# A transformer block with expert gather: four token groups of two blocks and a ring of ten tiles, in place of two groups of four and a ring of eight

## The chip, the cores and the metric

The kernel runs on one core of a Trainium2 chip. The metric is the device time of one execution in microseconds (us). PE is TensorE (matmuls; PEld are its weight loads), DVE is VectorE, ACT is ScalarE, POOL is GpSimd, SP is SyncE, which only issues DMAs here. All work is in float32.

## The reference

One transformer layer over 1024 tokens of width 1024, with two sub-layers and a final norm:

```python
h = modulate(rmsnorm(x, g1), shift1, scale1)          # shift, scale, gate from silu(c) @ w_ada
qa, ka, va, qb, kb, vb, ga, gb = split(h @ w_in)
y_sb = stick_breaking_attention(qa, ka, va)           # 8 heads of 64, strictly causal over all 1024
y_sw = sliding_window_sink_attention(qb, kb, vb, sinks)   # 8 heads, this chunk of 64 and the one before
x = x + gate1 * ((sigmoid(ga) * (y_sb @ sb_proj) + sigmoid(gb) * (y_sw @ sw_proj)) @ w_out)

h2 = modulate(rmsnorm(x, g2), shift2, scale2)
sub_s = (h2 @ w_q) . sub_keys                          # 8 heads x 2 halves x 128 keys
experts = top16 of the 16 x 16 sums of both top16s     # 16 of 16384 experts, per head and token
act = gelu(h2 . u[experts]); w = softmax(score) * act
x = x + gate2 * sum(w * v[experts])                    # 8 x 16 = 128 experts per token
out = rmsnorm(x, g_final)
```

Each token reads 128 rows of u and of v (2048 floats together) from a table of 16384 rows in HBM.

## The kernel before

**The gather stream.** Tokens lie in 8 blocks of 128. A block needs 128 gather tiles, 1024 in all. One tile is an indirect DMA on POOL (L498) which brings 128 rows of 2048 floats (1.05 MB: four experts each of 32 tokens) into one of the RING = 8 slots of a ring in SBUF. DVE multiplies the u half with the replicated h2 rows and sums (L1336), ACT applies gelu to two tiles' results (L1053), DVE multiplies with the softmax weight (L1347) and spreads it to a diagonal (L1350), PE adds the weighted v half into the block's output (L844), which frees the slots: POOL waits for `vs_done` before it fills a slot again. At a block's end the result goes through the final norm (L1361 to L1371), and the next block's h2 is replicated (PE L831, ACT L1046).

**The mixer.** Everything up to the scores of the sub-keys is done per group of tokens, GROUPS = 2 groups of GB = 4 blocks (T = 512 tokens). The stages of a group: H (norm and transposes, L531), V (L543), for each of 4 head pairs QK (L651) and then SB, one step per block of keys from the group's last block down to block 0, with both heads of the pair (PE L664, ACT abs, exp, ln at L985 to L995, DVE L1220 and L1237, PE L679 and L684, ACT exp L1003, PE L693, ysb copy L1015); SWP (projections of the sliding window, L724 to L739) and SW (L758 to L785, per block); MG (gates and merge, 8 slices of weights, L567 and L570); OUT (L596, per block, with the second norm and its transposes L580); PREP (queries and scores of the sub-keys, one step for each of 8 heads, L632 and L616). The scores go to HBM, and the selection of the top 16 (`keys`, DVE L1252 to L1312, four chunks of two heads per block) reads them from there; it is published through PE L813 and ACT L1030 and L1032 as the indices of 32 tiles.

Weights stream from HBM once per group. By the arrays' shapes: w_v 2 MiB, w_qk 4 x 1, w_sw 3, the table of slopes 0.75, w_mg 8 x 1.5, w_out 4, w_q 8 x 1 and sub-keys 8 x 0.125, and five broadcast rows of 0.5: 37.25 MiB (39 MB) per group. Three thirds of w_ada (8 MiB each) are read once, in the first group.

**The order.** Every engine runs one queue in order. Its instructions are merged when the kernel is built: each stream (`mixer(g)`, `keys`, `dot_products`, `sums`, ...) yields a due time before each piece, and `interleave` takes the earliest. The unit of due times is one gather tile: tile i is due at i. `Plan` gives the mixer's pieces their due times from costs in us, divided by a rate (1.9 us of mixer work per tile). Group 0 is placed before tile 0 (its PREP starts at -40), group 1 starts at tile 40. By these formulas group 1 has H at 40, V at 54, the first QK at 69, SWP at 231, SW at 258, MG at 291, OUT at 384, PREP from 432 to 508; its scores are first needed for block 4, whose tiles start at 512. ACT holds one set of functions at a time: gelu, exp with ln, and sqrt are three sets, and `Tables.use` (L92) loads another one where the next piece in the merged order needs it.

## Time and profile before

| | |
|---|---|
| median of 3 runs | 3839.58 us (3836.57 to 3844.09) |
| the profiled execution | 3838.94 us |
| its span, first to last instruction | 3837.1 us |
| busy: PE, DVE, POOL, ACT | 2710.1, 2223.6, 1172.6, 718.3 us |
| moved by DMA | 1235.07 MB, mean 322 GB/s |
| gather tiles | 1024 |
| loads of an ACT function set | 182 |

The profiled execution lies 1.8 us above its span and 0.6 us under the median. In the rows further down, a time is in us from the start of the span; "idle before" names what an engine was waiting for; PEclk is the granted TensorE clock as a share of 2.4 GHz; a matmul in float32 shows as two passes, each of them counted. A busy PE need not be at its peak, since ends of matmuls are modelled.

### The profile page before, as it was taken

What the parts mean: (1) busy time and instruction counts of PE and PEld (TensorE: products, weight loads), DVE (VectorE), ACT (ScalarE), POOL (GpSimd) and SP (SyncE); (2) the same over time, 40 slices, a digit from 0 to 9 for tenths busy, and PEclk for the clock granted to TensorE, in tenths of its full rate; (3) what the DMA queues carried; (4) which work ended last, traced back from release to release, by engine and by line L of the source; (5) the groups of instructions that cost most, each with busy time, mean ns of one, the idle gap of its engine ahead of it and who ended that gap; (6) DMA issues with size and microseconds to landing.
All of it is one profiled execution on the core that took longest, in us unless ns stands there. A gap on an engine that the chain in (4) does not pass through costs nothing. (4 is left out here: it accounts for less than half of the span.)

```text
span 3837.1 us, 33329 instructions
## 1 busy us (share of the span) xinstructions
PE 2710.1 (71%) x10216; PEld 879.3 (23%) x10216; DVE 2223.6 (58%) x5731; ACT 718.3 (19%) x1681; POOL 1172.6 (31%) x1033
## 2 busy tenths in 40 slices
PE   4886988877776777867998789655555555555555
PEld 2334433322221222222332233200110110001010
DVE  1113002458664667677776856677767767776755
ACT  1222001211435445131012211200010010001000
POOL 0000000133231333323433333444434434443443
PEclk8987999987898989988999899876777777778777
DMA  6310232699876878969998999999989989998998
GB/s 251 137 61 0 86 119 92 226 388 349 325 304 232 342 282 330 408 247 382 420 419 371 418 379 421 361 421 418 412 325 421 417 352 404 421 412 335 421 421 347
DMA packets 189067, 1235.07 MB, mean 322 GB/s; under 512 B 20348, under 2 KB 34716, under 8 KB 50392
## 3 DMA queue, kind: packets, MB, share of 16 engines
q0 software_dynamic: 147616, 1074.03, 69.2%
q1 hardware_dynamic: 41272, 158.91, 10.7%
q8 instruction: 81, 1.33, 0.1%
q14 instruction: 98, 0.80, 0.1%
HBM read 1208.71 MB, written 24.14 MB: 321 GB/s over the span
## 5 line engine op out<-in xcount | busy, mean ns | idle before, releaser
L498 POOL DMA_INDIRECT arena<-in_uv,idx_r x1024 | 1169.5, 1142 | 2639.3 <-PE pb L844 1727.9
L844 PE MATMUL pb<-arena,dg 128*32 128x512 f32 x4096 | 1288.2, 762 | 826.9 <-DVE dg L1350 826.5
L1336 DVE CUSTOM_DVE_ANT_0 arena<-arena 128x1024 f32<-128x1024 f32 x1024 | 1252.0, 1225 | 423.4 <-DMA arena<-in_uv,idx_r 398.2
L844 PEld LDWEIGHTS pb<-arena,dg 128*32 128x32 f32 x4096 | 225.9, 126 | 1780.3 <-DVE dg L1350 1251.3
L1053 ACT ACTIVATE gl<-dots 128x2 f32<-128x2 f32 x512 | 104.0, 203 | 1830.8 <-DVE dots L1336 1829.8
L1347 DVE TENSOR_TENSOR wv<-gl,gate_r 128x2 f32<-128x2 f32 x512 | 82.1, 160 | 336.2 <-ACT gl L1053 316.3
L92 ACT ACT_TABLE_LOAD x182 | 233.5, 1283 | 175.9 <-DVE dots L1336 142.1
L632 PE MATMUL pb<-arena 128*128 128x512 f32 x512 | 239.5, 614 | 12.0 <-issue 6.0
L567 PE MATMUL pb<-arena 128*128 128x512 f32 x512 | 233.2, 606 | 11.2 <-DMA arena<-in_w_mg 11.2
L831 PE MATMUL pb<-arena,ident 128*32 128x256 f32 x1024 | 98.6, 444 | 79.7 <-ACT arena L1046 75.9
L651 PE MATMUL pb<-arena 128*128 128x512 f32 x256 | 120.9, 622 | 19.3 <-DMA arena<-in_w_qk 19.3
L1220 DVE SCALAR_TENSOR_TENSOR arena<-pb,arena 128x512 f32<-128x512 f32 (+3 forms) x96 | 49.0, 552 | 139.7 <-ACT arena L995 132.1
L596 PE MATMUL pb<-arena 128*128 128x512 f32 x256 | 119.4, 617 | 14.7 <-DMA arena<-in_w_out 12.6
L632 PEld LDWEIGHTS pb<-arena 128*128 128x128 f32 x512 | 95.2, 195 | 150.1 <-issue 142.9
L567 PEld LDWEIGHTS pb<-arena 128*128 128x128 f32 x512 | 95.6, 192 | 145.4 <-issue 145.4
L1350 DVE TENSOR_TENSOR dg<-istack,wv 128x64 f32<-128x64 f32 x512 | 115.6, 226 | 19.4 <-DVE wv L1347 1.6
L1181 DVE SCALAR_TENSOR_TENSOR arena<-arena,pb 128x512 f32<-128x512 f32 x32 | 22.0, 687 | 180.9 <-PE pb L570 180.9
L570 PE MATMUL pb<-arena 128*128 128x512 f32 x256 | 116.1, 602 | 0.0
L679 PE MATMUL pb<-arena,tri 128*128 128x512 f32 (+3 forms) x192 | 85.1, 533 | 3.3 <-DVE arena L1220 3.3
L1252 DVE MAX8 vals<-arena 128x8 f32<-128x128 f32 x128 | 37.0, 289 | 84.5 <-DMA arena<-s_scratch 84.4
L1336 DVE DVE_READ_ACCUMULATOR2_ANT dots<- 128x1 f32 x1024 | 84.5, 83 | 0.0
L724 PE MATMUL pb<-arena 128*128 128x512 f32 x128 | 62.4, 640 | 17.7 <-DMA arena<-in_w_sw 17.7
(153 smaller groups left out, 2111.3 us busy)
## 6 DMA issues: line engine op xcount, KB each, us to landing
arena<-in_w_ada SPq DMA_DIRECT2D x12, 2048.0 KB, 17.5
arena<-in_w_mg SPq DMA_DIRECT2D x16, 1536.0 KB, 10.1
arena<-in_w_q SPq DMA_DIRECT2D x16, 1024.0 KB, 12.4
arena<-in_uv,idx_r POOLq DMA_INDIRECT x1024, 11.9
arena<-in_x SPq DMA_DIRECT2D x16, 512.0 KB, 13.5
arena<-in_w_qk SPq DMA_DIRECT2D x8, 1024.0 KB, 8.2
arena<-in_w_out SPq DMA_DIRECT2D x2, 4096.0 KB, 13.0
s_scratch<-arena SPq DMA_DIRECT2D x16, 512.0 KB, 15.3
```

Source lines behind the costliest of these rows:

```text
L92: self.act.add_instruction(mybir.InstLoadActFuncSet(name=self.nc.get_next_instruction_name(), act_func_set_id=table, engine=mybir.EngineTy ...
L498: pool.indirect_dma_start(ring[:, i % RING, :], None, uv, bass.IndirectOffsetOnAxis(ap=idx_r[:, b % 2, 4 * n + c:4 * n + c + 1], axis=0)). ...
L567: m = pe.matmul(bank, wmg[ft % 2][:, q * KT + k, :], hT[:, k, :], start=(k == 0), stop=(k == KT - 1))
L570: m = pe.matmul(bank, wmg[ft % 2][:, 16 + (q - 2) * 4 + k, :], y[:, k, :], start=(k == 0), stop=(k == 3))
L596: m = pe.matmul(pb[:, BGB + 2 * (j % 2) + i, :], merged[:, k, j * P:(j + 1) * P], wout[:, k, i * HALF:(i + 1) * HALF], start=(k == 0), sto ...
L632: m = pe.matmul(pb[:, BGB + p, 0:T], wq[h % 2][:, p, k, :], h2T[:, k, :], start=(k == 0), stop=(k == KT - 1))
L651: m = pe.matmul(pb[:, BGB + i, 0:T], wqk[p % 2][:, i * KT + k, :], hT[:, k, :], start=(k == 0), stop=(k == KT - 1))
L831: x_ = pe.matmul(pb[32 * q:32 * q + 32, MISC, 256:512], selector(c), h2cur[:, 256 * i:256 * i + 256], start=True, stop=True)
L844: m = pe.matmul(pb[32 * c:32 * c + 32, VACC + i, :], dg[:, n // 2 % 2, c, :], ring[:, (2 * g + c % 2) % RING, D + i * HALF:D + (i + 1) * H ...
L1053: act.activation(gl[:, 2 * (g % 4):2 * (g % 4) + 2], dots[:, 2 * (g % 4):2 * (g % 4) + 2], ACT.Gelu).then_inc(gelu_done, 1)
L1336: dve.tensor_tensor_reduce(u, h2rep[:, c, :], u, 1.0, 0.0, ALU.mult, ALU.add, dots[:, i % 8:i % 8 + 1]).then_inc(dots_done, 1)
L1350: dve.tensor_tensor(dg[:, n // 2 % 2, 2 * (n % 2):2 * (n % 2) + 2], istack[:].unsqueeze(1).to_broadcast([P, 2, 32]), w.unsqueeze(2).to_bro ...
```

## The change

The tokens are cut into four groups of two blocks (256 tokens), the ring gets 10 slots, and the plan gets a rate for each group and a start for each: group 0 again ahead of tile 0 (its head 2 of PREP at -36), the others at tiles 0, 230 and 480, at 2.2 us of mixer work per tile in place of 1.9. The buffers of a group get the size of 256 tokens. All matmuls whose moving side is the group's tokens (L567, L570, L632, L651, L724, L731) and the ACT and DVE work on their results are 256 wide in place of 512. Every group reads its own copy of the weights, so they are read four times. Keys are stored and read back for all earlier groups. The selection of chunk m is due as soon as head 2m+1 of PREP is through. STEP = 2 gives the gather stream the pairs of tiles that it has already.

```diff
-GROUPS = 2
-GB = NB // GROUPS
-T = GB * P
-
-RING = 8
+SIZE = (2, 2, 2, 2)
+GROUPS = len(SIZE)
+FIRST = [sum(SIZE[:g]) for g in range(GROUPS + 1)]
+GROUP = [g for g in range(GROUPS) for _ in range(SIZE[g])]
+GMAX = max(SIZE)
+TMAX = GMAX * P
+RATES = (1.9, 2.2, 2.2, 2.2)
+
+RING = 10
...
+STEP = 2
+STEPS = TILES // STEP
...
 def steps_of(g):
     out = []
-    for s in reversed(range(GB * (g + 1))):
-        lo = max(s * P - g * T, 0)
-        out.append((s, lo, s >= GB * g))
+    for s in reversed(range(FIRST[g + 1])):
+        lo = max(s - FIRST[g], 0) * P
+        out.append((s, lo, s >= FIRST[g]))
     return out
...
             for p in range(PAIRS):
-                self.item("QK", g, p, 16)
+                self.item("QK", g, p, 16 * part)
                 for i, (s, lo, diag) in enumerate(steps_of(g)):
-                    self.item("SB", g, (p, i), 2 + 6 * (T - lo) / T)
-                self.now += 3
+                    self.item("SB", g, (p, i), 2 + 6 * (SIZE[g] * P - lo) / 512)
+                self.now += 2
...
-        probe = Plan(1.9, [0, 0])
-        length = probe.at["PREP", 0, 0] - probe.at["H", 0, 0]
-        at = Plan(1.9, [-length - 40, 40.0])
+        probe = Plan([0] * GROUPS)
+        at = Plan([-probe("PREP", 0, 2) - 36, 0.0, 230.0, 480.0])
...
         def topk_at(b, m):
             n = CHUNKS * b + m
-            ready = at("PREP", b // GB, 2 * m + 2, 5) if m < 3 else at("PREP", b // GB, 7, 16)
+            ready = at("PREP", GROUP[b], 2 * m + 1, part(GROUP[b], 11) + 4)
             return ready if n < 2 else max(32.0 * (n - 2), ready)
...
                         if g:
-                            sp.wait_ge(k_st, 16 * PAIRS)
-                            sp.dma_start(kT[:, 0:g * T], k_dram[p]).then_inc(in_kA, 16)
-                        elif p < PAIRS:
-                            yield at("QK", g, p, 10)
+                            sp.wait_ge(k_st, 16 * PAIRS * g)
+                            sp.dma_start(kT[:, 0:FIRST[g] * P], k_dram[p, :, 0:FIRST[g] * P]).then_inc(in_kA, 16)
+                        if g + 1 < GROUPS:
+                            yield at("QK", g, p, part(g, 8) + 1)
                             sp.wait_ge(qk_act, 2 * n + 2)
-                            sp.dma_start(k_dram[p], kT[:, 0:T]).then_inc(k_st, 16)
+                            sp.dma_start(k_dram[p, :, FIRST[g] * P:FIRST[g + 1] * P], kT[:, FIRST[g] * P:FIRST[g + 1] * P]).then_inc(k_st, 16)
...
                             if i >= RING:
-                                pool.wait_ge(vs_done, (i - RING) // 2 + 1)
+                                pool.wait_ge(vs_done, (i - RING) // STEP + 1)
...
-                interleave(modulation(), publish(), replicate(), sums(), mixer(0), mixer(1))
+                interleave(modulation(), publish(), replicate(), sums(), *[mixer(g) for g in range(GROUPS)])
```

By the new formulas PREP of group 0 runs from -45.5 to -5.6. The other groups, in tiles:

| | H | V | QK 0 | SWP | SW | MG | OUT | PREP | end |
|---|---|---|---|---|---|---|---|---|---|
| group 1 | 0 | 6.6 | 14.0 | 70.2 | 83.1 | 97.8 | 137.8 | 162.2 | 196.9 |
| group 2 | 230 | 236.6 | 244.0 | 318.4 | 331.3 | 346.0 | 386.0 | 410.4 | 445.1 |
| group 3 | 480 | 486.6 | 494.0 | 586.5 | 599.5 | 614.2 | 654.2 | 678.5 | 713.3 |

## Rows read from the trace of the kernel before

**Rows 1.** Page, rate of all DMA in 40 slices of 96 us.
```profile
GB/s 251 137 61 0 86 119 92 226 388 349 325 304 232 342 282 330 408 247 382 420 419 371 418 379 421 361 421 418 412 325 421 417 352 404 421 412 335 421 421 347
```
**Rows 2.** Waits by engine and line: total us, times, longest.
```profile
POOL arena L498 <- ACT idx_r L1030: 714.1, 1, 714.1
```
**Rows 3.** The gathers' line: ns min/median/max, first and last start.
```profile
L498 POOL DMA_INDIRECT arena<-in_uv,idx_r x1024: 932/938/1990, 718.2 to 3811.1; - x171
```
**Rows 4.** Windows by stage: length, busy and (count) per engine, PEclk, DMA share, GB/s.
```profile
718.00:860.00 142.00, 115.33 (x508) 43.60 (x507) 77.14 (x220) 24.96 (x60) 49.25 (x44) 0.93 0.93 366
860.00:979.00 119.00, 76.04 (x256) 24.53 (x256) 90.16 (x236) 17.50 (x40) 37.21 (x32) 0.77 0.93 359
979.00:1564.00 585.00, 425.22 (x1625) 126.78 (x1626) 362.32 (x964) 268.31 (x478) 180.87 (x162) 0.88 0.79 303
1564.00:1657.00 93.00, 82.23 (x410) 32.62 (x411) 48.61 (x124) 13.98 (x39) 26.80 (x24) 0.95 0.85 349
1657.00:1775.00 118.00, 68.26 (x424) 29.64 (x424) 99.68 (x240) 40.70 (x115) 40.07 (x36) 0.80 0.82 303
1775.00:2064.00 289.00, 273.86 (x984) 92.11 (x984) 191.22 (x495) 33.71 (x93) 108.00 (x92) 0.99 0.97 404
2064.00:2212.00 148.00, 118.79 (x387) 37.98 (x386) 123.32 (x303) 29.69 (x60) 58.95 (x50) 0.90 1.01 419
2212.00:2432.00 220.00, 207.54 (x744) 77.86 (x744) 136.42 (x360) 29.93 (x76) 83.76 (x74) 0.96 0.99 403
2432.00:3811.00 1379.00, 773.24 (x3036) 141.57 (x3038) 952.33 (x2494) 137.00 (x417) 582.81 (x510) 0.75 0.97 396
```
**Rows 5.** Timeline of PE before the first gather: start, length, work [idle before].
```profile
29.18 9.71 PE L514 MATMUL pb<-arena,cb 128*32 128x512 f32 x64 [29.18 <-DMA arena<-in_w_ada]
51.03 1.94 PE L531 MATMUL pb<-ident,arena 128*128 128x128 f32 x8 [12.13 <-DVE arena L1109]
79.83 20.33 PE L543 MATMUL pb<-arena 128*128 128x512 f32 x47
106.89 17.05 PE L651 MATMUL pb<-arena 128*128 128x512 f32 x32 [6.73 <-DMA arena<-in_w_qk]
277.57 30.77 PE L724 MATMUL pb<-arena 128*128 128x512 f32 x64 [10.49 <-DMA arena<-in_w_sw]
323.04 1.16 PE L758 MATMUL pb<-arena 64*128 64x128 f32 x16 [0.69 <-ACT arena L897]
392.98 15.65 PE L567 MATMUL pb<-arena 128*128 128x512 f32 x32 [7.04 <-DMA arena<-in_w_mg]
572.26 28.06 PE L596 MATMUL pb<-arena 128*128 128x512 f32 x59 [12.57 <-DMA arena<-in_w_out]
650.23 16.72 PE L632 MATMUL pb<-arena 128*128 128x512 f32 x32 [5.92 <-DMA arena<-in_sk]
```
**Rows 6.** Timeline of ACT, first SB pair: last exps of two steps.
```profile
128.76 0.46 ACT L1003 ACTIVATE arena<-pb 128x128 f32<-128x128 f32 x2
133.51 0.66 ACT L1003 ACTIVATE arena<-pb 128x256 f32<-128x256 f32 x2
```
**Rows 7.** Waits in the window 979 to 1564 (SB of group 1).
```profile
POOL arena L498 <- PE pb L844: 374.9, 76, 21.8
DVE wv L1347 <- ACT gl L1053: 136.8, 52, 17.6
DVE arena L1336 <- DMA arena<-in_uv,idx_r: 16.2, 14, 2.6
```
**Rows 8.** Loads of function sets: page's group, then ACT's timeline.
```profile
L92 ACT ACT_TABLE_LOAD x182 | 233.5, 1283 | 175.9 <-DVE dots L1336 142.1 <-PE pb L567 14.9 <-DVE best L1305 6.9
...
1242.64 1.14 ACT L995 ACTIVATE arena<-arena 128x512 f32<-128x512 f32 x2
1243.81 1.28 ACT L92 ACT_TABLE_LOAD   x1
1245.10 0.20 ACT L1053 ACTIVATE gl<-dots 128x2 f32<-128x2 f32 x1
```

More of the change, by code:

```diff
@@ L156, in __call__ @@
     def __call__(self, stage, g, i, later=0.0):
-        return self.at[stage, g, i] + later
+        return self.at[stage, g, i] + later * RATES[0] / RATES[g]
 def build(nc, x, c8, w_ada, b_ada, g1, g2, gf, w_v, w_qk, w_sw, sinks, w_mg, w_out, w_q, sk, uv, consts,
@@ L253, in build @@
         skt = [rows(W0 + 4096 + 256 * i, 2, NKEYS) for i in range(2)]
-        qp = rows(W0 + 4608, 2, T)
-        ssb = [f(W0 + 5632 + 1024 * i, 1024).rearrange("p (b q n) -> p b q n", b=GB, q=2) for i in range(2)]
+        qp = rows(W0 + 4608, 2, TMAX)
+        ssb = [f(W0 + 4608 + 2 * TMAX * (i + 1), 2 * TMAX).rearrange("p (b q n) -> p b q n", b=GMAX, q=2) for i in range(2)]
         dve_steps, pool_steps = sem("dve_steps"), sem("pool_steps")
@@ L474, in finals @@
                         sp.dma_start(out[b * P:(b + 1) * P, :], yfin).then_inc(stored, 16)
-                interleave(start(), mods(), mixer(0), parked(0), keys(), blocks(), finals(), mixer(1), parked(1))
+                interleave(start(), mods(), mixer(0), parked(0), keys(), blocks(), finals(), *[s for g in range(1, GROUPS) for s in (mixer(g), parked(g))])
                 sp.wait_ge(stored, 16 * NB)
@@ L622, in mixer @@
                         for p in range(2):
-                            yield at("PREP", g, h, 4 * p)
+                            yield at("PREP", g, h, part(g, 4 * p))
                             if p == 0:
@@ L835, in sums @@
                     for b in range(NB):
-                        for n in range(PAIRS_OF_TILES):
-                            g = PAIRS_OF_TILES * b + n
-                            yield TILES * b + 2 * n + 1.8
+                        for n in range(STEPS):
+                            g = STEPS * b + n
+                            first = STEP * n % 4
+                            yield TILES * b + STEP * (n + 1) - 0.2
                             pe.wait_ge(dg_done, g + 1)
@@ L951, in mixer @@
                         for p in range(2):
-                            yield at("PREP", g, h, 4.5 + 3.2 * p)
+                            yield at("PREP", g, h, part(g, 4 + 4 * p) + 0.2)
                             act.wait_ge(pr_q, 2 * n + p + 1)
@@ L955, in mixer @@
                                 act.wait_ge(pr_s, 2 * n + p - 1)
-                            act.activation(qp[:, p, :], pb[:, BGB + p, 0:T], ACT.Copy).then_inc(pr_qe, 1)
-                        yield at("PREP", g, h, 9.5)
+                            act.activation(qp[:, p, 0:T], pb[:, BGB + p, 0:T], ACT.Copy).then_inc(pr_qe, 1)
+                        yield at("PREP", g, h, part(g, 8.5) + 1)
                         for p in range(2):
@@ L1063, in final @@
                         act.activation(stats[:, 50:51], stats[:, 49:50], ACT.Sqrt).then_inc(fin_rstd, 1)
-                interleave(start(), gates(), replicate(), gelus(), final(), mixer(0), mixer(1))
+                interleave(start(), gates(), replicate(), gelus(), final(), *[mixer(g) for g in range(GROUPS)])
             @block.vector
@@ L1371, in final @@
                         dve.scalar_tensor_tensor(out=yfin, in0=yfin, scalar=stats[:, 50:51], in1=final_row, op0=ALU.mult, op1=ALU.mult).then_inc(fin_done, 1)
-                interleave(start(), mods(), dot_products(), weights(), keys(), final(), mixer(0), mixer(1))
+                interleave(start(), mods(), dot_products(), weights(), keys(), final(), *[mixer(g) for g in range(GROUPS)])
 def shape_constants():
```

331 lines of the change are left out of this document (177 added, 154 removed).

## The prediction

> **What bounds the kernel now.** I read first the row of the gathers [rows 3]: they run from 718.2 to 3811.1, and 26 us after the last one starts the span is over. So the time has two parts, a start of 718 us without any gather and a stream of 1024 tiles in 3093 us, 3.02 us each. POOL waits once for the first indices, 714 us, and never again for indices [rows 2]; what it waits for afterwards are slots that PE frees. Then the rate of the DMA in slices [rows 1]: it stands at 0 to 251 GB/s ahead of the gathers, between 232 and 388 up to 1500, and touches 421 many times behind that. I take 421 as what the queues can carry; a tile of 1.05 MB is 2.49 us at that rate. Then the windows by stage [rows 4], the main view. Without any mixer (2432 to 3811) 510 tiles take 1379 us, 2.70 each, at a DMA share of 0.97. Beside MG, OUT and PREP the share is 0.97 to 1.01 too: 3.14, 2.96 and 2.97 us a tile, the surplus being the weights that use the same queues. Beside SB it is 0.79 and a tile takes 585 / 162 = 3.61 us; there something else is the bound. In that window POOL waits 375 us for slots, but DVE only 16 us for data that has not landed, and 137 us for a gelu [rows 7]. The tiles are there; DVE, ACT and PE pass a pair of tiles around in order, and the mixer's pieces stand in the same three queues.
>
> **The start.** Group 0 is now two blocks. Its stages before, from the timeline of PE [rows 5], with the idle time for weights taken out, and after:
> - H and V: 51.0 to 100.2, 49.2 us for four blocks; half is 24.6, so they end at 75.6. The first transposes at 51.0 wait for the modulation and stay. Wait for w_qk 6.7: 82.3.
> - SB: 106.9 to 267.1, 160.2 us. Two thirds of w_ada are worked in between, about 7.2 us each (the first third took 9.7), so a pair took 36.4. A pass of 512 columns takes 20.33 / 47 = 0.43 us, QK's 32 passes 13.8, and the four steps 22. After: 7 for QK at half the width, and the two narrow steps. The 256-wide step's last exp comes 4.75 us after the 128-wide one's [rows 6]; I take 10.5 for both with their ends. Four pairs of 17.5 and 14.4: 84.4, so 166.7; wait for w_sw 10.5: 177.2.
> - SWP 45.5, half 22.7. SW 62.9, half 31.5. Wait for w_mg 7. MG 166.7, half 83.4. Wait for w_out 12.6. We are at 334.4.
> - OUT 72, half is 36, with 5 more for the end of the last block, which does not halve. Wait for w_q 5.9: 381.
> - From 650.2 to the first gather at 718.2 are 68 us: two heads (34) and the way of the scores through HBM, selection and publishing (34). The heads halve: 17 + 34 = 51.
> The first gather starts at 433, 285 us earlier. Bounds: 415 (all waits for weights hidden by smaller stages) and 460 (passes of 256 columns bound by their weight loads, or a granted clock as low as 0.77, which [rows 4] shows where PE has less to do).
>
> **The stream: where mixer stands beside it.** By the due times groups 1 to 3 cover 197, 215 and 233 of the tiles, 645 in all, where group 1 covered 468 before; 379 tiles are free of mixer in place of 516.
> - Free: 379 x 2.70 = 1025 us.
> - MG, OUT, PREP: 40, 24.4 and 34.7 tiles per group. They are bound by bytes: MG 41.9 MB of tiles and 12.6 of w_mg with half a MB beside, 55 MB, 131 us at 421; before, the same account gives 278 of 289 us with the w_out that is read at its end, so 4% more: 137. OUT 25.6 of tiles, 4.2 of w_out and 4.7 of rows, x and results, 34.5 MB: 82. PREP 36.4, 9.4 of weights and 2.7 of scores, 48.5 MB: 115. Together 334 per group. PE has its half-wide passes and its own tiles beside them, some 118 us in MG: close behind the DMA, not ahead.
> - H, V, SWP and SW: 41.6 tiles per group. Before 330 us passed there for 92 tiles [rows 4], 3.6 each; I take 3.67 for the denser mixer: 153 (bounds 3.5 and 4.1 us a tile, 146 and 171). So 487 per group, 1461 for three.
> - SB: 56, 74 and 93 tiles, 223. Here is the one large unknown, for 256-wide steps beside gathers are in no row. The number of steps goes from 32 (most of them 512 wide) to 16 + 24 + 32 = 72, of at most 256. In group 0 the pair's 22 us for four steps of 320 columns on average are 5.6 each; I put a 512-wide step at 7 and a 256-wide one at 4.5 (4.75 in [rows 6]). If the mixer's chain and the tiles' chain stand behind one another, then before 585 = 162 a + 32 x 7 + 4 x 14, a = 1.88 us for a tile. After: 223 x 1.88 + 72 x 4.5 + 12 x 7 = 827. To that come the function sets.
> - Function sets: a tile's gelu between the mixer's exps costs a load before it and one behind it. Walking the merged order of ACT by its due times I count 182 loads before, as the page shows, and 263 after, about 160 of them beside SB (94 before; 0.58 a tile, now 0.72). The rise per tile is 0.14 x 1.28 us [rows 8], 40 us in all. SB: 867 us, 3.9 a tile. Lower bound 3.6 a tile, as before, 803; upper 4.3, if a 256-wide step costs no less than 5.6, 960.
>
> In the rows a load of 1.28 us starts 0.03 us behind the exp before it has ended, and the gelu starts as it ends [rows 8]. The Trainium skill (ScalarE: Activation LUTs, What ACT_TABLE_LOAD costs) states a drain of 1380 ns on top of the 1283 ns, 2.66 us for every switch. The 81 added loads would be 215 us of ACT by it and 104 by the row; the trace shows the 1283 and no drain, so the measurement decides and nothing of the page is in my sum.
>
> **Fill.** Chunk 1's selection now stands on DVE ahead of the first dot product, and the 16 replications of h2 behind its publishing. The first two slots come free some 45 us after the first gather, while ten slots cover 27: 18 us lost, and 2 for the last heads of PREP. Before, 142 us for 44 tiles [rows 4] were 23 more than 2.70 each. I take 20 (bounds 5 and 45).
>
> **Ring.** Ten slots help where the stream wants data: beside SB hardly at all (16 us of waiting [rows 7]). In the free part the DMA share of 0.97 leaves 3 to 4% of 1025 us, 40 at most, with as much again in all gaps beside MG and PREP. Value 25, bounds 0 and 60.
>
> **What is read more.** Two more groups are 78 MB of weights, 4 MB of keys and values read back: 82 MB, 195 us at 421. They are inside the 334 and the other terms. It is this that eats most of the 285 us, for where the queues are full a byte more is time more.
>
> **Sum.** 433 + 20 + 867 + 1461 + 1025 - 25 + 26 = 3807 of span, 3809 with the 1.8 us around it, against 3838.9 of the profiled execution (0.6 us under the median): 0.8% faster.
>
> **Rivals.**
> - *The overhead goes with the mixer's time, not with bytes* (faster). Group 1 took 1572 us for 470 tiles, 301 more than at 2.70; alone, as group 0, the same work took 724 us with its waits: 0.42 each. After, three groups are 3 x 313 + 408 = 1347 us of such work: 560. Then 433 + 20 + 1024 x 2.70 + 560 - 40 + 26 = 3764, 3766 with the rest. For it: shorter stages leave gaps for the weights. Against it: shares of 0.97 to 1.01 beside MG, OUT and PREP [rows 4], where no gap is left.
> - *Small steps are not cheap beside gathers* (slower than before). Place: the chain gelu, exp, sums between ACT, DVE and PE in SB. A step has eight ACT instructions and several hand-overs whatever its width, and each can be held by a gelu that waits for dots. At 4.3 us a tile SB is 960, and with H, V, SWP and SW at 4.1 a further 54 for three groups: 3809 + 93 + 54 = 3956; with one of the two, about 3902. It turns the sign once SB passes 867 + 30, 4.0 us a tile. For it: DVE already waits 137 us for gelus [rows 7]. Against it: ACT is busy for 268 of 585 us only.
> - *The gathers do not start earlier as planned*, or a group comes late: then POOL waits for indices once more. In the order of PE the first publishing stands behind five and a half heads of PREP (8.4 us each, 46), not later than the 51 above, and every group ends 30 tiles or more ahead of its block. Each 30 us of such waiting are 30 us of time; with 100 us it ends near 3905.
>
> **Chances.** Forecast 0.40 (its own range 3775 to 3850), faster rival 0.28, slower rival 0.27, late start or late group 0.05. Within 0.2% of the time before is about what a measurement can't tell from no change. Of the forecast's 0.40 some 0.27 lie below that band, 0.07 in it, 0.06 above: faster 0.55, same 0.07, slower 0.38. The range reaches from 3715, under the faster rival with the ring at its upper bound, to 3930, the slower one with one and a half of its two parts.
>
> **What would show it.** The first gather near 433; one long wait for indices and no second; SB at 3.9 us a tile in three windows; MG, OUT and PREP at a DMA share near 1 with 3.3 to 3.4 us a tile; 1317 MB moved; 263 loads of 1.28 us; free stretches at 2.65 a tile. Wrong would be above all the price of SB or of the bytes: a DMA share well under 0.95 beside MG and PREP would say that the bytes were not the bound.

## The result: slower by 1.2%

The changed kernel takes 3887.67 us in the median of three runs (3881.58 to 3889.43), 1.012 of the kernel before, with a 95% interval of 1.0097 to 1.0144: 48 us slower, where 30 us faster was forecast. The profiled run took 3889.43 us at a span of 3887.6.

The page of the changed kernel, its share and rate of the DMA in 40 slices of 97 us (the view of [rows 1]), then the group of the gathers and that of the function-set loads:

```profile
DMA  6324659989899968889899976889999999998998
GB/s 259 157 81 152 254 205 364 357 331 396 345 390 409 421 238 337 336 331 372 323 389 420 420 284 257 336 337 350 370 382 386 410 415 370 421 421 357 421 421 336
DMA packets 203460, 1318.25 MB, mean 339 GB/s; under 512 B 22172, under 2 KB 41148, under 8 KB 58872
...
L98 ACT ACT_TABLE_LOAD x263 | 337.4, 1283 | 173.6 <-DVE dots L1371 121.0
```

POOL's waits, and the gathers' own row (the views of [rows 2] and [rows 3]):

```profile
POOL arena L524 <- PE pb L874: 2057.7, 474, 62.6
POOL arena L524 <- ACT idx_r L1062: 443.3, 1, 443.3
...
L524 POOL DMA_INDIRECT arena<-in_uv,idx_r x1024: 932/937/1986, 447.4 to 3854.8; - x171
```

The stream starts 271 us earlier than before, as the change means it to, and its 1024 tiles take 3407 us in place of 3093. One wait for indices, 263 loads of function sets and 1318 MB are what the forecast said; so the program is the one I reckoned with, and its pace is not. One wait of POOL for a slot lasts 62.6 us; the longest in the kernel before was 21.8.

Windows by stage (the view of [rows 4]), each from the first pass of PE for one stage to the first pass for the next. Here are the first gathers, H and V of group 1, the merge (MG) of groups 1 and 3, OUT, SB of groups 2 and 3, and the free end:

```profile
447.00:513.00 66.00, 40.51 (x256) 22.57 (x256) 20.14 (x67) 14.45 (x36) 9.47 (x10) 0.68 0.65 257
513.00:570.00 57.00, 35.07 (x105) 11.45 (x105) 38.11 (x104) 4.37 (x12) 16.77 (x14) 0.77 0.77 292
...
859.00:1023.00 164.00, 138.11 (x705) 83.22 (x705) 96.12 (x257) 22.54 (x64) 41.31 (x40) 0.95 0.92 368
1023.00:1104.00 81.00, 60.42 (x209) 20.34 (x210) 48.25 (x113) 12.67 (x26) 25.17 (x24) 0.86 1.00 395
...
1362.00:1646.00 284.00, 208.26 (x1032) 92.38 (x1032) 165.16 (x462) 150.27 (x326) 79.71 (x74) 0.89 0.80 302
...
2261.00:2617.00 356.00, 258.67 (x1233) 115.64 (x1232) 214.31 (x599) 202.89 (x422) 101.96 (x92) 0.88 0.78 294
...
2708.00:2870.00 162.00, 136.92 (x705) 83.31 (x706) 97.37 (x257) 22.31 (x64) 42.62 (x40) 0.95 0.94 379
...
3059.00:3855.00 796.00, 444.75 (x1741) 82.39 (x1741) 558.10 (x1440) 75.57 (x238) 345.30 (x306) 0.77 0.99 405
```

The count behind POOL's time is the number of gathers (one that straddles an edge is counted on both sides). A tile costs 4.1 us beside the merge (before 3.14), 3.4 beside OUT (2.96), 3.75 beside SB (3.61), and 2.61 in the last stretch without a mixer (2.70). Term by term, in us; "over" is the time beyond 2.70 us for each tile of the term, which lets terms with different numbers of tiles be compared:

| term | forecast, over | measured, tiles, over |
|---|---|---|
| start, to the first gather | 433 | 447 |
| fill, to group 1's first pass | 20 over | 66, 10, 39 |
| H, V, SWP, SW of three groups | 459, 122 | 452, 129, 103 |
| MG of three groups | 411, 87 | 501, 121, 174 |
| OUT | 246, 48 | 243, 72, 49 |
| PREP | 345, 64 | 313, 90, 70 |
| SB | 867, 265 | 832, 222, 232 |
| free tiles, with the ring | 1000, -23 | 1001, 379, -22 |
| tail | 26 | 33 |

In the forecast the fill is a surplus alone, and its ten tiles stand in the other terms. The largest miss is the merge, 87 us over. SB, the one large unknown and the place of the slower rival, came out cheaper than reckoned.

### The profile page after: what moved, and what is told of

The parts are those of the page before. It is cut to its first block and busy times, and to the rows that moved or that the text cites. A ratio compares the mean times of both kernels' runs of the same rounds, so it can differ in the third digit from the quotient of the medians.

```text
span 3887.6 us, 38783 instructions
## 1 busy us (share of the span) xinstructions
PE 2726.6 (70%) x12392; PEld 1274.9 (33%) x12392; DVE 2233.1 (57%) x5887; ACT 869.2 (22%) x2156; POOL 1155.3 (30%) x1033
## 5 line engine op out<-in xcount | busy, mean ns | idle before, releaser
L524 POOL DMA_INDIRECT arena<-in_uv,idx_r x1024 | 1152.2, 1125 | 2700.3 <-PE pb L874 2057.7
L874 PE MATMUL pb<-arena,dg 128*32 128x512 f32 x4096 | 1225.8, 732 | 686.2 <-DVE dg L1386 681.4
L98 ACT ACT_TABLE_LOAD x263 | 337.4, 1283 | 173.6 <-DVE dots L1371 121.0
L659 PE MATMUL pb<-arena 128*128 128x256 f32 x1024 | 251.1, 401 | 55.2 <-issue 36.1
L594 PE MATMUL pb<-arena 128*128 128x256 f32 x1024 | 248.1, 396 | 19.1 <-DMA arena<-in_w_mg 19.1
L659 PEld LDWEIGHTS pb<-arena 128*128 128x128 f32 x1024 | 199.9, 200 | 112.6 <-issue 78.6
L594 PEld LDWEIGHTS pb<-arena 128*128 128x128 f32 x1024 | 196.5, 197 | 89.0 <-issue 62.4
L679 PE MATMUL pb<-arena 128*128 128x256 f32 x512 | 133.6, 419 | 71.5 <-DMA arena<-in_w_qk 71.5
L623 PE MATMUL pb<-arena 128*128 128x512 f32 x256 | 123.9, 634 | 59.0 <-DMA arena<-in_w_out 59.0
L679 PEld LDWEIGHTS pb<-arena 128*128 128x128 f32 x512 | 104.6, 210 | 113.5 <-DMA arena<-in_w_qk 75.5
L1255 DVE SCALAR_TENSOR_TENSOR arena<-pb,arena 128x256 f32<-128x256 f32 (+1 forms) x160 | 56.1, 392 | 136.7 <-ACT arena L1027 112.3
L1215 DVE SCALAR_TENSOR_TENSOR arena<-arena,pb 128x256 f32<-128x256 f32 x64 | 27.0, 421 | 169.1 <-PE pb L597 168.9
L597 PE MATMUL pb<-arena 128*128 128x256 f32 x512 | 119.0, 383 | 0.0
L707 PE MATMUL pb<-arena,tri 128*128 128x256 f32 (+1 forms) x320 | 102.3, 412 | 3.4 <-DVE arena L1255 2.8
L597 PEld LDWEIGHTS pb<-arena 128*128 128x128 f32 x512 | 95.9, 190 | 25.4 <-issue 13.0
L721 PE MATMUL pb<-arena 128*64 128x256 f32 (+1 forms) x320 | 71.2, 428 | 37.5 <-ACT arena L1035 37.3
## 6 DMA issues: line engine op xcount, KB each, us to landing
arena<-in_w_ada SPq DMA_DIRECT2D x12, 2048.0 KB, 17.4
```

The costliest lines, as they stand in the source:

```text
L98: self.act.add_instruction(mybir.InstLoadActFuncSet(name=self.nc.get_next_instruction_name(), act_func_set_id=table, engine=mybir.EngineTy ...
L524: pool.indirect_dma_start(ring[:, i % RING, :], None, uv, bass.IndirectOffsetOnAxis(ap=idx_r[:, b % 2, 4 * n + c:4 * n + c + 1], axis=0)). ...
L594: m = pe.matmul(bank, wmg[ft % 2][:, q * KT + k, :], hT[:, k, 0:T], start=(k == 0), stop=(k == KT - 1))
L597: m = pe.matmul(bank, wmg[ft % 2][:, 16 + (q - 2) * 4 + k, :], y[:, k, 0:T], start=(k == 0), stop=(k == 3))
L623: m = pe.matmul(pb[:, BGB + 2 * (j % 2) + i, :], merged[:, k, j * P:(j + 1) * P], wout[:, k, i * HALF:(i + 1) * HALF], start=(k == 0), sto ...
L659: m = pe.matmul(pb[:, BGB + p, 0:T], wq[h % 2][:, p, k, :], h2T[:, k, 0:T], start=(k == 0), stop=(k == KT - 1))
```

## Two views that the forecast had not used

**What PE does in a merge.** The costliest groups of PE in the window 2708 to 2870 of the changed kernel, and in 1775 to 2064 of the kernel before (busy, mean ns | idle before, releaser):

```profile
L594 PE MATMUL pb<-arena 128*128 128x256 f32 x256 | 63.4, 398 | 4.1 <-DMA arena<-in_w_mg 4.1
L874 PE MATMUL pb<-arena,dg 128*32 128x512 f32 x160 | 38.2, 598 | 4.8 <-DVE dg L1386 4.8
L597 PE MATMUL pb<-arena 128*128 128x256 f32 x128 | 30.0, 382 | 0.0
L623 PE MATMUL pb<-arena 128*128 128x512 f32 x1 | 1.2, 1219 | 15.0 <-DMA arena<-in_w_out 15.0
```

```profile
L567 PE MATMUL pb<-arena 128*128 128x512 f32 x256 | 120.3, 612 | 4.1 <-DMA arena<-in_w_mg 4.1
L844 PE MATMUL pb<-arena,dg 128*32 128x512 f32 x376 | 89.2, 598 | 5.4 <-DVE dg L1350 5.4
L570 PE MATMUL pb<-arena 128*128 128x512 f32 x128 | 59.9, 612 | 0.0
```

In the change PE is busy 137 us of that merge's 162 and stands 25, of them 15 at its end (4 more lie just ahead of it). Before it was 274 us busy and stood 15 in 289. I had read the DMA share of 0.97 there and a bytes account of 278 us, and called the merge bound by bytes; PE's account fits as well. The standing at the end is new. In both kernels w_out goes where hT lies and is read only when the merge's passes are over. Before, 34 us of other passes and short waits lay between the merge's last pass and OUT's first, and PE never stood for w_out beside the gathers; in the change 20 us lie there in this merge, and PE stands some 15 us in every group.

**For what PE stands at the edges of stages.** PE's waits for loads between 447 and 3900 us in the changed kernel, and in 718 to 3811 of the kernel before (total, times, longest):

```profile
PE pb L679 <- DMA arena<-in_w_qk: 51.6, 3, 18.4
PE pb L623 <- DMA arena<-in_w_out: 45.2, 3, 15.2
PE pb L753 <- DMA arena<-in_w_sw: 27.3, 3, 9.9
PE pb L659 <- DMA arena<-in_sk: 12.7, 1, 12.7
PE pb L594 <- DMA arena<-in_w_mg: 12.6, 3, 7.7
```

```profile
PE pb L651 <- DMA arena<-in_w_qk: 12.5, 1, 12.5
PE pb L724 <- DMA arena<-in_w_sw: 7.3, 1, 7.3
PE pb L567 <- DMA arena<-in_w_mg: 4.1, 1, 4.1
```

149 us against 24. Why the one for w_qk is the longest shows in the timeline of the change ahead of group 2's SB (start, length, engine):

```profile
1342.92 0.69 DVE L1151 COPY arena<-pb 128x512 f32<-128x512 f32 x1 [4.84 <-PE pb L570]
1343.63 0.37 SPq L388 DMA_DIRECT2D v_scratch<-arena  x1
1344.05 0.51 SPq L399 DMA_DIRECT2D arena<-in_w_qk  x1
...
1362.42 2.08 PE L679 MATMUL pb<-arena 128*128 128x256 f32 x4 [17.70 <-DMA arena<-in_w_qk]
```

SP issues w_qk in the order in which the mixer is written, behind the stores of V, and the last of these waits for DVE's copy at 1342.9, the end of V. From its issue the 1 MB load takes 18.3 us. It stands behind that store in the queue too: the store of 256 KB, in packets of 512 bytes, lands 14.1 us after its issue at 1343.6, and packets of w_qk move only from 1357 on. SP's own wait for the store shows it:

```profile
SPq L405 <- DMA v_scratch<-arena: 13.2, 1, 13.2
```

The gathers alone don't make the 18 us: at 1344 three to four of them were issued and not yet moved, and in e9 below, where w_qk goes ahead of V's stores, the same load lands after 9.1 us with as many gathers on the way.

## Experiments

Ratios are to the kernel before on the same chip, with their 95% intervals; 0.1% is 3.8 us. The change itself stands at 1.012 (1.0097 to 1.0144). Runs that differ from it by less than some 0.4% have intervals that meet its own. In e4, e6, e7, e8, e11 and e12 one wait of DVE in the selection of the top 16 also stands one instruction earlier.

**Ring and bytes.** e1: `RING = 10` to `8`. e2 adds to it:

```diff
+                def extra():
+                    for k in range(40):
+                        yield 4.0 + 13 * k
...
+                        sp.dma_start(f(E0 + 2048 * (k % 2), 2048), w_mg[k % 8, :, 0:2048]).then_inc(in_extra[k % 2], 16)
```

> The changed kernel with a ring of 8 tiles in place of 10, nothing else. The forecast gave the ring 25 us (theory: two more tiles in flight carry the gathers over the points where the queue waits on PE's gather sums). If that term is right: 3888 + 25 = 3913 us. Rival: 8 tiles of 1 MB already cover every wait, the ring is worth nothing: 3883 to 3893 us.

> The kernel of the run before (ring of 8) with 40 extra reads of 1.05 MB each from w_mg into a spare buffer that nobody uses, one every 13 tiles through tiles 4 to 511, the stretch in which the mixers of groups 1 to 3 run. It prices bytes alone: 42 MB more, no engine work. Theory bytes: the stream of gathers is bound by bytes there, 42 MB at 421 GB/s = +100 us over the ring of 8. Theory chain: beside the mixers the in-order chain of PE and DVE sets the time (DMA share .78 to .94 in these windows), and the extra bytes go into the gaps: +30 us or less. A result of 50 to 80 us would say that about half of the tiles are bound by each.

e1: 1.0156 (1.0136 to 1.0177), 14 us over the change; the intervals meet, so the ring is worth between nothing and some 25 us. In the profiled runs it is 17: 22 in the free stretches, where the forecast had put it, less 5 of tail, for with ten slots the last gathers end later behind the last issue. e2: 1.027 (1.0244 to 1.0297), 44 us for 42 MB (31 to 57 by the intervals) in place of 100 or 30, on average 1.05 us a MB, less than half of what it takes at 421 GB/s (2.4). By this average the 83 MB of the change would be 87 us, not the 195 I had said.

The average hides two prices. The merges of groups 1 and 2, in e1 and then in e2, which issues 8 of its reads there:

```profile
853.00:1017.00 164.00, 138.42 (x704) 83.38 (x704) 91.04 (x244) 22.34 (x63) 40.32 (x40) 0.95 0.92 368
1746.00:1922.00 176.00, 143.66 (x736) 84.83 (x735) 89.53 (x242) 26.01 (x68) 43.75 (x41) 0.91 0.86 345
```

```profile
856.00:1024.00 168.00, 138.91 (x705) 83.91 (x706) 92.58 (x248) 22.48 (x64) 39.97 (x40) 0.94 0.95 382
1772.00:1950.00 178.00, 143.12 (x736) 84.09 (x736) 90.25 (x243) 25.91 (x68) 44.25 (x41) 0.92 0.88 356
```

That is 6 us for 8.4 MB, 0.7 us a MB; in SB it is 3 us for 14 reads. In PREP and the free stretch behind it, at a DMA share of 0.97 to 1.01, the same two groups go from 422 to 455 us for 12 reads, 2.6 us a MB. So the bytes bind where the forecast's share was near 1 outside the merge, and hardly in the merge itself (one profiled run of each kernel).

**The fill.**

```diff
-        at = Plan([-probe("PREP", 0, 2) - 36, 0.0, 230.0, 480.0])
+        at = Plan([-probe("PREP", 0, 2) - 36, 10.0, 230.0, 480.0])
```

> The changed kernel with group 1 beginning at tile 10 in place of tile 0; ring of 10. In the trace of the change 10 gathers were issued from 447.4 to 458.7, and then the queue stood until 522.2, since group 1's norm stands ahead of the first dot product on DVE. Theory stall: with the norm behind the first ten tiles, the 53 us for the first ten gathers become some 20: 3888 - 33 = 3855 us (3845 to 3865). Rival: the wait for the first x and for ACT's 16 replications is needed anyway, or comes back when group 1's norm is due at tile 10: 3883 to 3893 us.

1.0074 (1.0057 to 1.0091): 18 us less than the change. The timeline of the change shows the stall (POOL, then DVE):

```profile
458.72 0.94 POOL L524 DMA_INDIRECT arena<-in_uv,idx_r  x1 [0.30 <-issue]
522.24 0.93 POOL L524 DMA_INDIRECT arena<-in_uv,idx_r  x1 [62.58 <-PE pb L874]
```

```profile
484.57 0.17 DVE L1134 TENSOR_SCALAR stats<-stats 128x2 f32<-128x2 f32 x1 [16.09 <-ACT arena L898]
...
510.13 1.28 DVE L1142 SCALAR_TENSOR_TENSOR arena<-arena,stats 128x1024 f32<-128x1024 f32 x1 [25.19 <-ACT stats L903]
...
512.59 1.22 DVE L1371 CUSTOM_DVE_ANT_0 arena<-arena 128x1024 f32<-128x1024 f32 x1
```

Group 1's norm, due at tile 0, stands ahead of the first dot product, waits for an x that SP reads only after all of PREP, and then for a root that stands behind 16 replications on ACT. In e3:

```profile
497.88 0.94 POOL L524 DMA_INDIRECT arena<-in_uv,idx_r  x1 [40.21 <-PE pb L874]
```

A third of the wait goes (62.6 to 40.2); before, with 8 slots, it was 19.1. In e3 the first dot product waits for a replication, 12 us, but why the first slot comes free only 52 us after the first gather, where it took 30 before, no run separates.

**Density.** e4, e7 and e8 change the rates of groups 1 to 3 (`RATES`) to 1.9, 2.5 and 3.0, and their begins: 484 for the last group in e4, tiles 10, 240, 490 in e7 and 10, 260, 520 in e8. Group 1 at tile 10 alone gave 18 us (e3).

> The changed kernel with all four planned rates at 1.9, as the kernel before had, in place of 2.2 for groups 1 to 3 (the last group begins at tile 484 in place of 480; in the top-k one wait of DVE stands one instruction earlier). Each stage of groups 1 to 3 is spread over 16 per cent more tiles: some 253 tiles of mixer work beside the gathers become about 290, and the free tiles at the end shrink. Same bytes, same PE work. Theory density: merge and the other stages are bound by PE's passes in the order that the rates fix (3.95 us a tile in merge); with 16 per cent more tiles each stage takes hardly longer in all, and some 35 to 40 tiles of 2.6 us leave the free stretch, 3888 - 60 = 3828 us (3800 to 3850). Rival bytes: the time is bytes over rate wherever the mixers stand, 3880 to 3895 us.

> The changed kernel with planned rates of 2.5 in place of 2.2 for groups 1 to 3, begins at tiles 10, 240 and 490 (in the top-k one wait of DVE stands one instruction earlier). The run at rate 1.9 was 34 us slower: its windows show nearly the same 3.2 to 3.9 us a tile in every stage with 87 more tiles beside the mixers (730 in place of 643). Theory pace: what a tile beside a mixer costs hangs little on how much mixer work goes with it, so fewer tiles beside mixers is faster: at 2.5 some 566 are left, 77 fewer at .39 us each = -30 us, and the late begin of group 1 alone gave -17 us: 3888 - 17 - 30 = 3841 us. Rival saturation: at 2.2 PE is busy .87 of the merge and of PREP, so that from here each stage takes as long with fewer tiles: -17 us at most from the late begin, 3865 to 3875 us.

> As the run before, with planned rates of 3.0, begins at tiles 10, 260 and 520: some 475 tiles beside the mixers in place of 643. Theory pace: 168 tiles fewer at .39 us each = -66 us and -17 us from the late begin: 3805 us. Rival saturation: merge and PREP keep their time with fewer tiles, only SB, SWP and SW gain: 3840 to 3870 us. Rival collapse: the engines' queues get more mixer work between two gathers than the ring covers, and each mixer stage holds the gathers up: 3890 us or more.

e4: 1.020 (1.0182 to 1.0218), 31 us slower than the change. e7: 1.0275 (1.0245 to 1.0306). e8: 1.0439 (1.0409 to 1.0469). Both theories of e4 fell, and so did both that I then had for e7 (it is 59 us over the change); of e8's three the "collapse" came about, 123 us over the change. To read them I added up all windows with a mixer, from the first pass of one stage to that of the next, and took 2.70 us off for each tile:

| kernel, rate | tiles beside mixers | their time, us | over 2.70 a tile | of it MG |
|---|---|---|---|---|
| before, 1.9 (4 blocks) | 466 | 1546 | 288 | 41 |
| e4, 1.9 (6 blocks) | 724 | 2586 | 631 | 179 |
| change, 2.2 | 634 | 2341 | 629 | 174 |
| e7, 2.5 | 570 | 2252 | 713 | 195 |
| e8, 3.0 | 488 | 2084 | 766 | 233 |

From 1.9 to 2.2 the mixers cost the same in all; above it they cost more. Two of e8's windows of the merge:

```profile
815.00:964.00 149.00, 118.33 (x529) 80.40 (x530) 70.31 (x191) 11.90 (x38) 28.69 (x28) 0.89 0.82 331
...
2828.00:3000.00 172.00, 134.35 (x664) 83.72 (x664) 73.91 (x195) 21.44 (x59) 29.65 (x30) 0.88 0.72 283
```

Only 28 to 30 tiles, yet 149 to 172 us, and PE less busy than in the change: neither PE nor the DMA is at its limit. That they wait for each other is my reading, no run shows it. e4 is slower by 31 us (39 in the profiled runs), and its mixers have no part in it: over 2.70 us a tile its two short free stretches between the groups cost 18 us more than those of the change, and the last free stretch 15 more. The cause of both I don't know.

**What bounds the merge.** In e5 the gates contract 4 of 8 parts. A third of the merge's matmuls is left out, and the output is no longer the layer's:

```diff
                                 if q < 2:
-                                    m = pe.matmul(bank, wmg[ft % 2][:, q * KT + k, :], hT[:, k, 0:T], start=(k == 0), stop=(k == KT - 1))
+                                    if k < 4:
+                                        m = pe.matmul(bank, wmg[ft % 2][:, q * KT + k, :], hT[:, k, 0:T], start=(k == 0), stop=(k == 3))
```

> The changed kernel with the two gates of the merge contracting the first 4 of their 8 parts (8 of the merge's 24 blocks of matmuls are left out for every f, in all groups; the output differs). Loads, waits, dues and the 40 tiles beside each merge stay. It asks what bounds the merge: in the trace of the change PE is busy 137 to 143 us of its 158 to 169 us, and the DMA share is .87 to .94. It takes 128 passes of .22 us from each group = 28 us of PE. Group 0's merge lies before the gathers on PE alone: -28 us in the start under both theories. Theory PE's order: the three merges beside the gathers shrink by 25 to 28 us each: 3888 - 28 - 78 = 3782 us. Theory bytes (or anything else that goes per tile): they stay at 155 to 165 us: 3860 us.

0.9938 (0.9921 to 0.9954), 3821 us: between the two, 70 us under the change. The start gave 31 us (first gather at 416.5). The three windows from the first pass of SWP to the first of OUT, e5 and then the change:

```profile
729.00:978.00 249.00, 179.30 (x960) 96.95 (x960) 163.98 (x428) 45.97 (x135) 74.70 (x68) 0.89 0.92 370
1606.00:1863.00 257.00, 184.79 (x960) 97.84 (x959) 164.29 (x433) 46.43 (x135) 78.33 (x68) 0.86 0.90 360
2559.00:2797.00 238.00, 178.08 (x960) 96.78 (x960) 162.68 (x422) 45.96 (x133) 74.31 (x68) 0.90 0.96 385
```

```profile
761.00:1023.00 262.00, 207.03 (x1089) 121.91 (x1090) 164.99 (x429) 46.35 (x135) 73.39 (x68) 0.90 0.90 354
1646.00:1917.00 271.00, 211.09 (x1089) 121.93 (x1089) 165.12 (x434) 47.54 (x135) 75.24 (x68) 0.88 0.87 343
2617.00:2870.00 253.00, 205.30 (x1089) 121.75 (x1090) 165.51 (x426) 46.04 (x133) 73.92 (x68) 0.91 0.93 369
```

786 us become 744: 42 us for 81 us less of PE; the merges alone go from 501 to 464. So PE's time counts here by half, and a byte, by e2's windows, by less than a third of its 2.4 us a MB. The merge is not bound by bytes, as the forecast had it, nor by PE's passes alone.

**The code without the grouping.** `SIZE = (4, 4)`, rates 1.9, ring 8, second group from tile 40:

> The changed kernel with two groups of 4 blocks, rates 1.9, ring of 8 and the second group from tile 40: the grouping of before in the code of the change (which plans shorter pauses between stages; in the top-k one wait of DVE stands one instruction earlier). If the grouping, the ring and the rates are all that matters: the kernel before, 3835 to 3850 us. Rival: the shorter planned pauses or the moved due times of replication and parking cost something of their own, 3860 us or more; or they help, 3825 or less.

1.0023 (1.0011 to 1.0035), 9 us slower than before (4 to 13): grouping, rates and ring carry most of the change's 48 us, its other edits some 9. That lies between the two outcomes that I had expected.

**The standing of PE.** e9:

```diff
                     sp.dma_start(f(W0, 4096), w_v).then_inc(in_wv, 16)
+                    yield at("V", g, 0, 1)
+                    sp.wait_ge(h_rows, FIRST[g + 1])
+                    sp.dma_start(wqk[0].rearrange("p a n -> p (a n)"), w_qk[0]).then_inc(in_wqk[0], 16)
...
-                    sp.dma_start(f(W0, 6144), w_sw).then_inc(in_wsw, 16)
+                    sp.dma_start(f(W0, 2048), w_sw[:, 0:2048]).then_inc(in_wsw, 16)
+                    sp.dma_start(f(W0 + 2048, 4096), w_sw[:, 2048:6144]).then_inc(in_wsw2, 16)
```

and w_out likewise in two halves of its columns. e10 is e9 with group 1 at tile 10, e14 the same with the early w_qk alone, e15 is e14 with the keys of earlier groups read ahead of the wait for V's stores, e16 is e10 with that.

> The changed kernel with three loads of weights placed so that PE stands less: a group's first w_qk is issued ahead of the stores of V (before, behind the last of them, which waits for DVE), and w_sw and w_out come in two parts each, PE waiting for the first part alone. Same bytes, same matmuls. In the trace of the change PE stood 51.6 us for w_qk, 45.2 us for w_out and 27.3 us for w_sw in 9 waits beside the gathers (in the kernel before 12.5 us for w_qk and 7.3 us for w_sw, one wait each). Some 80 of these 124 us should go, and some 10 us of the start. Theory PE's order: what PE stands is made up by nobody in the stages that PE's chain sets; by the cut merge, where half of the removed PE time came back, -40 -10 = 3838 us. Rival bytes: while PE stands the gathers go on landing, nothing but the start gains: 3875 to 3885 us.

> The run before with group 1 beginning at tile 10 in place of 0, which alone gave 17 us. If the two gains are independent: 17 us below the run before, 3821 us by the theory of PE's order, 3860 by bytes. It also says whether four groups can beat the kernel before (3840) at all.

> The change with the early w_qk and group 1 at tile 10, but w_sw and w_out loaded whole as in the change. In the trace of the run that split them, PE stood as long for w_out as before (45.5 us) and half as long for w_sw (12.6 in place of 27.3 us), and the windows of SWP, SW and OUT kept their length. Theory: all of the gain is w_qk's: 3814 us as with the splits (3810 to 3820). Rival: the splits gave 10 us or more: 3825 us.

> The run before with the keys of earlier groups (k_scratch) of a group's first pair loaded ahead of the wait for V's stores, in place of behind it. With w_qk early, PE stands 40 us in 3 waits for k_scratch, which had been hidden behind the wait for w_qk. Theory PE's order: some 10 us a group of it go and the time with them: 3814 - 25 = 3789 us. Rival: the values (v_scratch, behind V's stores) are late next, and PE stands for these: 3805 to 3815 us.

> Four groups with all that the runs gave: w_qk early, w_sw and w_out in two parts, k_scratch ahead of V's stores, group 1 at tile 10. The run without the last-but-one item stood at .9954 of the kernel before, and that item gave .001 where it was tried: .994 to .995 expected (some 3820 us where before takes 3840). If the splits bring nothing (their 10 us were within the intervals of two runs): .997.

e9: 0.9996 (0.9986 to 1.0006), 48 us less than the change and at 3838 us by the ratio, where the theory of PE's order had it; e10: 0.9954 (0.9938 to 0.9971), the two gains add. H and V of groups 2 and 3, from their first pass to QK's, in the change and in e9:

```profile
1307.00:1362.00 55.00, 32.71 (x106) 11.04 (x104) 37.51 (x93) 3.23 (x11) 18.79 (x16) 0.81 1.02 421
2205.00:2261.00 56.00, 32.84 (x105) 11.33 (x106) 35.07 (x94) 2.99 (x10) 20.14 (x16) 0.80 1.01 416
```

```profile
1275.00:1313.00 38.00, 32.98 (x106) 11.15 (x104) 29.19 (x75) 2.84 (x9) 15.31 (x14) 0.89 1.01 420
2159.00:2197.00 38.00, 31.94 (x105) 10.89 (x105) 29.41 (x81) 3.10 (x10) 14.82 (x14) 0.93 1.02 421
```

With group 1, 168 us for 46 tiles become 116 for 40: 36 us beyond 2.70 a tile; the first gather comes 12 us earlier, which makes the 48. A DMA share of 1.0 had not meant that the stretch was bound by bytes. While PE stood, the queues worked off what had been issued: in the change POOL issues no gather from 1348 to 1372, and from 1363 to 1373 the DMA share is 0.08. The waits of PE that e9 leaves:

```profile
PE pb L630 <- DMA arena<-in_w_out: 45.5, 3, 15.7
PE pb L699 <- DMA arena<-k_scratch: 40.1, 3, 16.4
...
PE pb L762 <- DMA arena<-in_w_sw: 12.6, 3, 5.0
```

The first half of w_out lands no earlier than the whole did (17.4 to 18.0 us after its issue, the second half after 22.3 to 22.8; the whole after 16.8 to 18.2); w_sw's wait is halved; k_scratch takes w_qk's place. Over 2.70 us a tile SWP, SW, MG and OUT cost 278 us in e9 and 283 in the change, so the splits hardly show there. e14, 0.9979 (0.9964 to 0.9995), lies 10 us over e10, but the intervals meet, so what the splits are worth is between nothing and some 18 us. e15, 0.9969 (0.9952 to 0.9986), shows no gain over e14 that can be told: PE now stands 36.5 us for v_scratch where it stood 41.6 for k_scratch, as the rival said. e16: 0.9947 (0.993 to 0.9964).

**Fewer groups, and the kernel before with its loads moved.** e11 and e12: `SIZE = (3, 3, 2)`, ring 8, without and with e9's edit. e13 and e17: the kernel before with the early w_qk, and with all of e9's edit.

> The code of the change with groups of 3, 3 and 2 blocks, rates 1.9, ring of 8, begins at tiles 10 and 396 (in the top-k one wait of DVE stands one instruction earlier). It asks whether the cost goes with the number of groups. Reckoned over a free tile (2.70 to 2.75 us), the mixers beside the gathers cost 289 us for 4 blocks in the kernel before (72 a block) and 623 us for 6 blocks in the change (104 a block). Theory (each group brings its own weights and its own standing of PE): 3 blocks a group lie between, 85 a block x 5 = 425 us; start some 580 us; 1024 x 2.75 = 2816 us; fill and tail 60 us beyond: 3850 to 3880 us less what the shorter stages of the start bring, best value 3855. Rival: the cost goes with the blocks beside the gathers alone (each 104): 580 + 2816 + 520 + 40 = 3956 us.

> The run before with the three loads of weights placed as in the run of the weights. It has two groups beside the gathers in place of three, so two thirds of that gain: by PE's order -30 us (3825 us if the grouping comes out at 3855), by bytes -8 us.

> The kernel before (two groups of 4, ring of 8) with a group's first w_qk issued ahead of the stores of V, and nothing else. The same move in the change was most of a gain of 56 us (windows: 13 us of the start, 36 us in H and V of three groups). In the kernel before PE stood 12.5 us for w_qk beside the gathers and 6.7 us in group 0. Theory (the standing of PE before QK comes once a group, so two groups have a third of it beside the gathers): 7 us of the start and some 10 us beside the gathers, 3831 - 17 = 3814 us, which is where four groups with the move came out. Rival: with four blocks V is long enough to hide it, 3825 to 3832 us, and four groups stay faster by 10 us or more.

> The kernel before with w_qk early and w_sw and w_out in two parts: two groups of 4, ring of 8. With w_qk early alone it stood at .9949. It decides, with the run beside it, whether four groups gain anything once the loads are placed alike. Theory (four groups carry some 3 blocks more of mixer work beside the gathers, and each its own weights; what they gain in the start is given back): this one is level with four groups or faster, .993 to .995. Rival: the splits cost where descriptors get shorter (w_out in rows of 2 KB), .996 or more.

e11: 1.0143 (1.0126 to 1.016), e12: 1.0019 (1.0001 to 1.0037), e13: 0.9949 (0.9933 to 0.9966), e17: 0.9937 (0.9924 to 0.9949). At 1.0143 (3895 us) three groups lie 40 us over the best value and no lower than four. By e11's windows a block beside the gathers costs 91 us over 2.70 a tile (457 for five), between 72 and 104 as the theory had it, where its sum had 85; the rival's 104 gave 3956 us and fell. What the sum lacked is the fill: 66 us over, up to group 1's first pass, where the change has 39. Its first gather comes at 572.6, 125 us later than in the change, and the stream gives back as much. Moving the loads gave three groups 48 us, not the 30 of two groups in three. e13 gives the kernel before 20 us, 11 of them by an earlier first gather (at 707.5 in its profile): its waits for w_qk were 12.5 and 6.7. With all loads moved, two groups stand at 0.9937 and four at 0.9947. Both beat both kernels of this case, and between them nothing can be told.

## Why the forecast was wrong

The span is 3888 us where the sum had 3807. Of the 81 us the start has 14, the merge 87, PREP 6, the tail 7 and SB -33, each over 2.70 us a tile; OUT and the free tiles are right within 1, and fill and H, V, SWP, SW together are right at 142. That these two cancel is luck: the fill is 19 too low, the other 19 too high, because its price came from a window of before that begins 20 us ahead of H's first pass.

- **Merge, +87. The failed step is "bound by bytes"**, 137 us a group with PE at 118 us "close behind the DMA". It measured 164, 175 and 162 us; PE was busy 137 to 143 and stood 25 in group 3, of it 15 for w_out. e2 and e5 show what took its place: a MB more costs 0.7 us in the merge in place of 2.4, and a us of PE less gives half a us. The bytes were short as well: the three windows moved 183 MB in place of 165, mostly w_out, which the sum had put into OUT; at 421 GB/s that is 436 us of the 501. (The same account does not give the 278 us of before either: 92 tiles, w_mg, w_out and half a MB are 114 MB, 270 us; the trace has 117 MB.) The forecast's own sentence on what would show it wrong, a DMA share well under 0.95 beside MG, has come true only in part (0.92, 0.87, 0.94).
- **Start.** 433 forecast, 447 measured, inside its bounds of 415 to 460. PREP began 12 us later than in the sum (392.7 for 381); 10 of these are group 0's SB, whose end the first pass of SWP marks (186.9 for 177.2).
- **Fill, +19.** I let the first slots come free 45 us after the first gather, by the selection and the replications; it was 75. Left out was group 1's H, due at tile 0 on DVE, ACT and SP, ahead of the first dot product. e3 gives back 18 us.
- **H, V, SWP, SW, -19.** Cheaper than forecast, though there was no wait for a load in my price beyond what the window of before held. w_qk's wait is per group, three in place of one and 17 us in place of 12.5: without it these stages would have been 36 us lower, by e9.
- **SB, -33.** 3.4, 3.8 and 3.9 us a tile, 3.75 in all, against 3.9: a 256-wide step is cheaper than the 4.5 us I put if the tile's 1.88 us hold, and the slower rival, which had the right sign, had the wrong place. Over 2.70 a tile SB costs 37 us a block before and 39 after.
- **Function sets.** 263 loads of 1283 ns, as counted. The Trainium skill (ScalarE: Activation LUTs, What ACT_TABLE_LOAD costs) states a drain on top of each load; by its figures an estimate for the 81 added loads is 215 us. No run here shows a drain, and SB came out under the sum without it.
- **Bytes, ring, tail.** 1318 MB as forecast. In PREP and the free stretches, where the share is near 1, they cost what the forecast said; in the merge and SB they don't. The ring is worth 14 of the 25, with a wide interval. The tail is 33 with ten slots and 27 with eight (e1).
- **The faster rival** (3766 us) had shorter stages leave gaps for the weights. The cheap bytes of the merge bear that out, but PE's passes alone, busy for 418 of the 501 us, left little to gain there.

Against the kernel before, the start gained 271 us, the stream lost 314 and the tail 7. Over 2.70 us a tile, by stage:

| | before (4 blocks) | change (6 blocks) |
|---|---|---|
| to group 1's first pass | 39 | 39 |
| H, V | 17 | 43 |
| SB | 147 | 232 |
| SWP, SW | 50 | 60 |
| MG | 41 | 174 |
| OUT | 12 | 49 |
| PREP | 20 | 70 |
| free tiles | 5 | -22 |

So 144 of the 314 us are two more blocks beside the gathers at the price of before (72 each), and some 198 are what the mixers of six blocks cost beyond that price: 112 in MG, 40 in PREP, 31 in OUT, 18 in H and V, 11 in SB, less 15 in SWP and SW; the free tiles give back 27. Six blocks at the price of before would read a copy and a half of a group's weights, and the change reads three. In PREP the difference is 14 MB of w_q and sub-keys, 34 us at 421 GB/s, and e2 shows that bytes count in full there. In MG it is 19 MB of w_mg, some 13 us at e2's 0.7; the three waits for w_out are 45 us, if they count in full, and the rest of the 112 is open. The account by stage is measured, the causes inside a stage are in part my reckoning. What it says is that the gain of the start was no more than its cost in the stream.

Open are e4's 33 us in the free stretches, why the first slot comes free so late, and what would be left of the merge's surplus without w_out's wait, which no run removed.

## What to carry to other kernels

Where a window shows two engines near their limit, make both accounts before you call it bound by one: here a us of PE counted for half and a MB for less than a third of its full price, and a forecast that took the bytes in full and PE at nothing was 87 us short. Price a change by stage: the average of 1.05 us a MB was 0.7 in the merge and 2.6 in PREP and behind it. Compare terms by their surplus over a common price of a tile, for the number of tiles in a term shifts. Splitting work into more groups repeats every wait at a stage's edge: list what the in-order engine stands for, load by load, multiply by the number of groups, and look in the issuing queue for a load that stands behind a store it doesn't need; here it waited for the store's data to be ready, and then for its packets to go. Try the same repair on the old kernel before crediting the new grouping with it.

## What the hardware showed that I had not expected

Two transfers of the same queue show it best. Behind a store of 256 KB in packets of 512 bytes, a load of 1 MB landed 18.3 us after its issue (16.2 to 19.0 in the three groups); ahead of that store it landed after 9.1 (7.2 to 9.1), with three to five gathers on the way in both cases. The store itself took 14.1 us beside the gathers (27 GB/s while the gathers moved 393) and 2.3 us in the kernel before ahead of the first gather. The first of two column halves of a 4.2 MB load ended no earlier than the whole (15.7 against 15.2 us of waiting at most).

A DMA share of 1.0 over 55 us turned into 38 us for the same passes when one load came earlier. And 42 MB more cost 44 us in a stream whose DMA share was some 0.8 to 1.0, most of it in the stretches where the share was at 0.97 or more.
